# The exact last step of a top-k selection cut into pieces between other VectorE work

## The chip, the cores and the metric

The kernel runs on one core of a Trainium2 chip. The metric is the device time of one execution in microseconds, the median over the runs. TensorE multiplies matrices (in the profile PE, its weight loads PEld), VectorE (DVE) and ScalarE (ACT) work elementwise, GpSimd (POOL) does little here, and SyncE (SP) issues most loads. Each engine works through its own instructions in the order in which they were written, and waits on semaphores for the others.

## The reference, cut to what matters

Two transformer blocks of 1024 tokens and width 1024. The change lies in the second block's mixer, whose four branches share one projection. Branches 0 and 1 are differential attention, branch 2 is a mixture of dilated attentions, branch 3 attends to the 256 keys that an indexer scores highest:

```python
def dsa_attention(q, k, v, iq, ik, iw, table):
    topk = min(TOPK_MAX, S // 4)                    # 256
    def block(args):                                # 128 queries
        logits = einsum('bqhd,bkd->bqhk', iqb, ik) * (IDX_DIM ** -0.5)
        score = einsum('bqhk,bqh->bqk', relu(logits), iwb)
        score = where(kpos <= qpos, score, NEG)
        _, idx = lax.top_k(score, topk)
        ...
        s = where(valid, q @ k[idx] * scale + bias, NEG)
        return softmax(s) @ v[idx]
```

Among equal scores top_k takes the lower index first, so the selection must be exact. For the queries of tiles 0 and 1 (of 128) every admissible key is taken; tiles 2 to 7 need the selection.

## The kernel before

The attention of the four branches is one loop of 64 steps, `for n in range(STEPS2 + 1)`, written once for each engine. Step n is branch n // 16, query tile t = (n % 16) // 2 and half x = n % 2; its scores are 128 x 128 (t + 1), twice (m = 0, 1). So steps 32 to 47 are branch 2 and steps 48 to 63 branch 3, and steps get wider from t = 0 to 7.

TensorE's step n: `scores2(n)` (L1070), `turn2(n - 1, 0)` (L1081, transposes of the weights), fillers, `turn2(n - 1, 1)`, fillers, `values2(n - 1)` (L1098). Fillers are matmuls of other work, put there by the table `fillers()`: projections (L992, L1003), the first half of the output projection (L1015, "out", steps 38 to 44), the memory's keys and values (L1030, L1040). A filler takes one of two PSUM banks, and its result must have been read before the bank is used again. For "out" it is VectorE that reads it (L2459, in `filled`), for the others ScalarE.

ScalarE's step n: copy of turn2(n - 1, 0), exp of (n, 0) in `weigh` (L1709), copy of fillers, copy of turn2(n - 1, 1), exp of (n, 1), and up to step 55 counts of signs for the search (L1756). All its copies are the helper's line L1279.

VectorE's step n: `scored(n, 0)`, `narrow("low")`, `scored(n, 1)`, `narrow("high")` (scored adds the bias and takes the maximum: L2412, or L2407 and L2409 with the selection; narrow is a pass of a search by halving), the fillers' additions of slot 0, `normalise(n, 0)` and `(n, 1)` (L2435 reciprocal, L2437), the additions of slot 1, then `keep_ranked(n)`.

The search finds for each row two neighbouring floats, between which the 256th score lies: tiles 2 to 5 ("low") by step 33, tiles 6 and 7 ("high") by step 56. `keep_ranked` is the exact last step of one tile: it counts the scores at least as large as the bound (`at least`) and larger (`beyond`), both in parts of 256 columns (L2348), derives the value and the number of equals still to be taken (L2350 to L2358), and for each part marks the equals, numbers them by a scan, keeps the first of them and adds those above (L2362 to L2370). L2373 turns the marks into an addend. The table

```python
RANKED_AT = {34: 2, 36: 3, 38: 4, 40: 5, 57: 6, 59: 7}
```

says at the end of which step which tile is done. The result of tile t is wanted by `scored` of step 48 + 2 t.

Of the kernel before, what the change touches and what calls it, by code (L numbers as in the profile page):

```python
# [211 lines left out]
RANKED_AT = {34: 2, 36: 3, 38: 4, 40: 5, 57: 6, 59: 7}  # L212
# [54 lines left out]
class Psum:  # L267
# [20 lines left out]
    def at(self, key):  # L288
        return self.tensor[:, self.bank[key] * 512:8 * 512]
# [48 lines left out]
def program(nc, A, known):  # L338
# [7 lines left out]
    steps = Steps(sems, known)  # L346
# [3 lines left out]
    at = steps.value  # L350
# [118 lines left out]
    def sel(t):  # L469
        return view(SEL_AT[t], (t + 1) * P)  # L470

    def vec(name, i=0, n=1):
        a = VEC0 + VCOL[name] + i
        return S[:, a:a + n]
# [1393 lines left out]
    def vector_program(raw):  # L1868
# [461 lines left out]
        def parts_of(t):  # L2330
            return [(a, min(256, (t + 1) * P - a)) for a in range(0, (t + 1) * P, 256)]

        def keep_ranked(n):

            if n not in RANKED_AT:
                return
            t = RANKED_AT[n]
            j, x, parts = t - 2, sel(t), parts_of(t)
            e.wait_ge(*at(("turned ends", "low" if t < 6 else "high")))
            if t > 2:  # L2340
                e.wait_ge(*at(("sel", t - 1)))
            for name, total, compare in (("at least", at_least, ALU.is_ge), ("beyond", beyond, ALU.is_gt)):
                for p, (a, w) in enumerate(parts):
                    if p:
                        e.wait_ge(*at((name, t, p - 1)))
                    elif name == "beyond":
                        e.wait_ge(*at(("at least", t, len(parts) - 1)))
                    v.tensor_scalar(equal[:, 0:w], x[:, a:a + w], above[:, j:j + 1], total if p else 0.0, compare, ALU.add,  # L2348
                                    accum_out=total).then_inc(*e.step((name, t, p)))
            v.tensor_scalar(is_above, at_least, float(TOPK), None, ALU.is_ge).then_inc(*e.step(("is above", t)))  # L2350
            e.wait_ge(*at(("beyond", t, len(parts) - 1)))
            v.tensor_tensor(beyond, at_least, beyond, ALU.subtract).then_inc(*e.step(("at bound", t)))
            v.tensor_scalar(at_least, at_least, -1.0, float(TOPK), ALU.mult, ALU.add).then_inc(*e.step(("left", t)))
            e.wait_ge(*at(("is above", t)))
            stt(out=rank_value, in0=gap[:, j:j + 1], scalar=is_above, in1=below[:, j:j + 1], op0=ALU.mult, op1=ALU.add).then_inc(
                *e.step(("rank value", t)))
            e.wait_ge(*at(("left", t)))
            stt(out=rank_left, in0=beyond, scalar=is_above, in1=at_least, op0=ALU.mult, op1=ALU.add).then_inc(*e.step(("rank left", t)))  # L2358
            e.wait_ge(*at(("rank left", t)))
            for p, (a, w) in enumerate(parts):  # L2360
                count = prefix[p % 2][:, 0:w]
                v.tensor_scalar(equal[:, 0:w], x[:, a:a + w], rank_value, None, ALU.is_equal).then_inc(*e.step(("equal", t, p)))  # L2362
                e.wait_ge(*at(("equal", t, p)))
                v.tensor_tensor_scan(count, equal[:, 0:w], equal[:, 0:w], prefix[(p - 1) % 2][:, 255:256] if p else 0.0,
                                     ALU.add, ALU.max).then_inc(*e.step(("prefix", t, p)))
                e.wait_ge(*at(("prefix", t, p)))
                stt(out=equal[:, 0:w], in0=count, scalar=rank_left, in1=equal[:, 0:w], op0=ALU.is_le, op1=ALU.mult).then_inc(
                    *e.step(("first equal", t, p)))
                e.wait_ge(*at(("first equal", t, p)))
                stt(out=x[:, a:a + w], in0=x[:, a:a + w], scalar=rank_value, in1=equal[:, 0:w], op0=ALU.is_gt, op1=ALU.add).then_inc(  # L2370
                    *e.step(("selected", t, p)))
                e.wait_ge(*at(("selected", t, p)))
            v.tensor_scalar(x, x, 1.0, -8 * NEG, ALU.subtract, ALU.mult).then_inc(*e.step(("sel", t)))  # L2373

        e.wait_ge(*at("iw"))
        for t, i in INDEX_STEPS:
            for m in range(2):
                h = 2 * i + m
                n = 8 * (t - 2) + h
# [16 lines left out]
        def scored(n, m):  # L2396

            br, t, x = step2(n)
            s = 8 * (n % 5) + 3 * m
            tile, ps, bias = score_tile(n, m), psum.at(("s2", n, m))[:, 0:(t + 1) * P], strip_of(n, m)  # L2400
            e.wait_ge(*at(("strip", br, x if br >= 2 else 0)))
            e.wait_ge(*at(("s2 mm", n, m)))
            if 2 * n + m >= 3:
                e.wait_ge(*at(free(*divmod(2 * n + m - 3, 2))))
            if br == 3 and t >= 2:
                e.wait_ge(*at(("sel", t)))
                v.tensor_tensor(tile, ps, bias, ALU.add).then_inc(*e.step(("biased", n, m)))  # L2407
                e.wait_ge(*at(("biased", n, m)))
                v.tensor_tensor_reduce(out=tile, in0=tile, in1=sel(t), scale=-0.125, scalar=3e38, op0=ALU.add, op1=ALU.min,  # L2409
                                       accum_out=small[:, s:s + 1]).then_inc(*e.step(("max2", n, m)))  # L2410
            else:
                v.tensor_tensor_reduce(out=tile, in0=ps, in1=bias, scale=-0.125, scalar=3e38, op0=ALU.add, op1=ALU.min,  # L2412
                                       accum_out=small[:, s:s + 1]).then_inc(*e.step(("max2", n, m)))
                steps.at["biased", n, m] = steps.at["max2", n, m]

        def combine(n):

            s = 8 * (n % 5)
            e.wait_ge(*at(("exp2", n, 0)))
            e.wait_ge(*at(("exp2", n, 1)))  # L2420
            v.reciprocal(small[:, s + 5:s + 6], small[:, s + 4:s + 5]).then_inc(*e.step(("recip sum2", n)))
            v.reciprocal(small[:, s + 2:s + 3], small[:, s + 1:s + 2]).then_inc(*e.step(("recips", n)))
            e.wait_ge(*at(("recip sum2", n)))
            v.tensor_scalar(small[:, s + 5:s + 6], small[:, s + 5:s + 6], small[:, s + 1:s + 2], neg_lam,
                            ALU.mult, ALU.mult).then_inc(*e.step(("ratio", n)))
            e.wait_ge(*at(("ratio", n)))
            p0 = score_tile(n, 0)
            stt(out=p0, in0=score_tile(n, 1), scalar=small[:, s + 5:s + 6], in1=p0, op0=ALU.mult, op1=ALU.add).then_inc(
                *e.step(("prob", n, 0)))

        def normalise(n, m):

            s = 8 * (n % 5) + 3 * m
            e.wait_ge(*at(("exp2", n, m)))
            v.reciprocal(small[:, s + 2:s + 3], small[:, s + 1:s + 2]).then_inc(*e.step(("recips", n, m)))  # L2435
            e.wait_ge(*at(("recips", n, m)))
            v.tensor_scalar(score_tile(n, m), score_tile(n, m), small[:, s + 2:s + 3], None, ALU.mult).then_inc(  # L2437
                *e.step(("prob", n, m)))
# [14 lines left out]
        def filled(kind, *which):  # L2453

            if kind == "out":
                m, c = which
                x = X[:, m, 512 * c:512 * c + 512]
                e.wait_ge(*at(("out2a mm", m, c)))
                v.tensor_tensor(x, psum.at(("out2a", m, c))[:, 0:512], x, ALU.add).then_inc(*e.step(("x2a", m, c)))  # L2459

        for n in range(STEPS2 + 1):
            if n < STEPS2:
                scored(n, 0)
            narrow("low", n - 1)
            if n < STEPS2:
                scored(n, 1)
            narrow("high", n - 1)
            for piece in FILLERS.get((n, 0), ()):
                filled(*piece)
            if n < 32:  # L2470
                combine(n)
            elif n < STEPS2:
                normalise(n, 0)
                normalise(n, 1)
            for piece in FILLERS.get((n, 1), ()):
                filled(*piece)
            if n == MEM_STEP:
                e.wait_ge(*at("mem rr"))
                for k in range(KD):
                    stt(out=mem[:, k, :], in0=mem[:, k, :], scalar=vec("norm_memkv", k), in1=mem_rr, op0=ALU.mult,  # L2480
                        op1=ALU.mult).then_inc(*e.step(("mem h", k)))
            keep_ranked(n)
            count_least(n)
            if 1 <= n <= 32:
                divide(n - 1)
# [283 lines left out]
    @block.vector  # L2769
    def _(raw):  # L2770
        vector_program(raw)
# [167 lines left out]
```

## Time and profile before

| | us |
|---|---|
| median of 3 runs | 3599.42 |
| lowest, highest | 3598.71, 3608.11 |
| the profiled execution | 3598.85 |
| its span in the trace | 3597.1 |
| TensorE busy | 3436.0 (96%) |
| VectorE busy | 1601.4 (45%) |
| ScalarE busy | 978.1 (27%) |

The profile is of one execution. A timeline row gives start, length, engine, line, operation, operands, the number of merged instructions, and in brackets the idle time of the engine before it and what ended it. The matmuls' ends are modelled; start to start is the surer measure. The loop's steps 32 to 63 lie at 2049 to 2397 us.

### The profile page before, as it was taken

The page shows a single profiled execution, that of the slowest core. Times are in us where ns is not written, and L with a number is a line of the kernel's source. Part 1 is how long each engine was busy: PE and PEld are TensorE (multiplying, and loading weights), DVE is VectorE, ACT ScalarE, POOL GpSimd, SP SyncE. Part 2 cuts the span into 40 slices and gives each one's busy share as a digit, 9 for nine tenths or more (in the row PEclk, how much of TensorE's full clock was granted, in tenths as well). Part 3 has the DMA queues.
Part 4 walks back from the last instruction along what each step waited for, and adds up shares of the span by engine and source line. Part 5 has one row for each costly group of instructions (what it writes and reads, how often), then busy time and mean ns, then how long its engine had stood idle before and what let it go on. Part 6 is the DMA issues. An engine that isn't in the chain of part 4 may idle for free.

```text
span 3597.1 us, 31176 instructions
## 1 busy us (share of the span) xinstructions
PE 3436.0 (96%) x12370; PEld 1812.8 (50%) x12370; DVE 1601.4 (45%) x2938; ACT 978.1 (27%) x2059; POOL 93.6 (3%) x107
## 2 busy tenths in 40 slices
PE   7999999999999999999999999899999999999998
PEld 3556555555456444544566455564444444444443
DVE  2056191143156362552465563654336555253433
ACT  4244112002244111122577744531111000000001
POOL 0000000020000000100000000000110000000000
PEclk9999999999999999999999999899999999999999
DMA  5100121131000101111000101111000111101011
GB/s 209 54 6 13 58 88 62 53 108 38 27 7 13 34 27 53 41 44 41 36 24 30 39 21 56 62 45 44 29 24 35 47 47 35 47 35 47 35 41 65
DMA packets 49903, 163.72 MB, mean 46 GB/s; under 512 B 5296, under 2 KB 8624, under 8 KB 49085
## 3 DMA queue, kind: packets, MB, share of 16 engines
q1 hardware_dynamic: 44890, 145.82, 11.5%
q10 hardware_dynamic: 4868, 15.91, 1.3%
q8 instruction: 98, 1.61, 0.2%
q14 instruction: 47, 0.39, 0.0%
HBM read 157.46 MB, written 11.32 MB: 47 GB/s over the span
## 4 chain that ended last, share of the span: by engine, by line
PE 86%; DVE 7%; ACT 4%; issue 1%; SPq 1%; DMA 0%; POOL 0%; DVEq 0%; ACTq 0%; POOLq 0%
PE ps L551 34%; PE ps L1220 14%; PE ps L580 8%; PE ps L992 5%; PE ps L708 4%; PE ps L1003 2%; PE ps L731 2%; PE ps L887 2%; PE ps L720 2%; PE ps L1015 1%; PE ps L1070 1%; ACT sb L1756 1%; PE ps L1081 1%; DVE sb L2000 1%; PE ps L977 1%; PE ps L1098 1%
## 5 line engine op out<-in xcount | busy, mean ns | idle before, releaser
L551 PE MATMUL ps<-sb 128*128 128x512 f32 (+1 forms) x3088 | 1240.9, 563 | 14.0 <-ACT sb L1559 6.7
L551 PEld LDWEIGHTS ps<-sb 128*128 128x128 f32 x3088 | 589.3, 191 | 659.3 <-issue 633.8
L1279 ACT ACTIVATE sb<-ps 128x512 f32<-128x512 f32 (+10 forms) x709 | 350.6, 511 | 1522.9 <-PE ps L551 467.3
L1220 PE MATMUL ps<-sb 128*128 128x512 f32 x1232 | 531.3, 594 | 2.8 <-DVE sb L2626 2.8
L1220 PEld LDWEIGHTS ps<-sb 128*128 128x128 f32 x1232 | 234.6, 191 | 299.0 <-issue 293.5
L580 PE MATMUL ps<-sb 128*128 128x512 f32 x672 | 291.4, 594 | 2.4 <-ACT sb L1279 1.9
L992 PE MATMUL ps<-sb 128*128 128x512 f32 x512 | 231.3, 599 | 0.0
L580 PEld LDWEIGHTS ps<-sb 128*128 128x128 f32 x672 | 127.3, 190 | 163.2 <-issue 156.1
L1321 ACT ACTIVATE sb<-sb 128x512 f32<-128x512 f32 x128 | 74.7, 610 | 366.0 <-DVE sb L2573 122.5
L2136 DVE SCALAR_TENSOR_TENSOR sb<-sb 128x1310 f32<-128x1310 f32 (+1 forms) x120 | 161.7, 1424 | 0.0
L708 PE MATMUL ps<-sb 96*128 96x512 f32 (+1 forms) x400 | 155.3, 523 | 5.2 <-ACT sb L1468 4.5
L1756 ACT ACTIVATE sb<-sb 128x384 int8<-128x384 f32 (+4 forms) x160 | 152.2, 953 | 2.4 <-DVE sb L2295 0.7
L992 PEld LDWEIGHTS ps<-sb 128*128 128x128 f32 x512 | 94.2, 192 | 107.3 <-issue 106.5
L2000 DVE TENSOR_REDUCE sb<-ps 128x1 f32<-128x1280 f32 (+1 forms) x72 | 98.8, 1372 | 97.4 <-PE ps L708 97.3
L2573 DVE TENSOR_TENSOR sb<-ps,sb 128x512 f32<-128x512 f32 x64 | 44.2, 691 | 216.7 <-PE ps L551 216.7
L1880 DVE SCALAR_TENSOR_TENSOR sb<-sb 128x512 f32<-128x512 f32 (+1 forms) x138 | 88.0, 704 | 110.8 <-ACT sb L1302 86.0
L1003 PE MATMUL ps<-sb 128*128 128x256 f32 x512 | 115.6, 381 | 0.0
L1709 ACT ACTIVATE sb<-sb 128x128 f32<-128x128 f32 (+7 forms) x128 | 98.7, 771 | 62.3 <-DVE sb L2412 33.1
L708 PEld LDWEIGHTS ps<-sb 96*128 96x128 f32 x400 | 71.9, 192 | 78.8 <-issue 73.2
L1003 PEld LDWEIGHTS ps<-sb 128*128 128x128 f32 x512 | 95.6, 190 | 18.0 <-issue 6.2
L720 PE MATMUL ps<-sb 128*128 128x128 f32 x656 | 99.5, 281 | 5.1 <-DVE sb L2017 2.1
L1468 ACT ACTIVATE sb<-ps,sb 128x1280 f32<-128x1280 f32 (+1 forms) x72 | 88.6, 1231 | 48.9 <-DVE sb L2000 48.7
(258 smaller groups left out, 3148.9 us busy)
## 6 DMA issues: line engine op xcount, KB each, us to landing
sb<-in_w_in SPq DMA_DIRECT2D x73, 512.0 KB, 3.3
sb<-in_w_ada SPq DMA_DIRECT2D x48, 512.0 KB, 4.6
sb<-in_w_up SPq DMA_DIRECT2D x44, 512.0 KB, 3.3
sb<-in_w_down SPq DMA_DIRECT2D x24, 384.0 KB, 3.1
sb<-in_w_out SPq DMA_DIRECT2D x16, 512.0 KB, 3.6
sb<-in_w_mkv SPq DMA_DIRECT2D x16, 512.0 KB, 3.3
rows_dram<-vec_dram ACTq DMA_DIRECT2D x1, 6906.0 KB
sb<-rows_dram ACTq DMA_DIRECT2D x6, 1024.0 KB, 5.1
```

The lines of the kernel that those rows point to most:

```text
L551: ins = mm(ps[:, 0:tn], w[:, k, :], src(k, t0, tn), start=(k == 0), stop=(k == nk - 1))
L580: ins = mm(ps[:, 0:512], stationary(k), moving(k), start=(first and k == 0), stop=(k == 3), skip_group_check=not first)
L708: ins = mm(ps[:, b:b + w], qh[0:96, h % 2, t * P:(t + 1) * P], kh[0:96, h, keys0 + b:keys0 + b + w], start=True, stop=True)
L720: ins = transpose(ps[:, (j - g) * P:(j - g + 1) * P], prob[u % 3][:, j * P:(j + 1) * P], ident)
L992: ins = mm(ps[:, 0:512], weights[name][:, k, :], H2[:, k, 512 * c:512 * c + 512], start=(k == 0), stop=(k == KD - 1))
L1003: ins = mm(ps[:, 0:256], H2[:, k, t * P:(t + 1) * P], w[k // 4][:, k % 4, :], start=(k == 0), stop=(k == KD - 1))
L1220: ins = mm(ps[:, 0:512], stationary(k), moving(k), start=(first and k == 0), stop=(k == 3), skip_group_check=not first)
L1279: return act(out, in_, func, scale=scale)
L1709: act(tile, tile, ACT.Exp, bias=small[:, s:s + 1], scale=-1.0, accum_out=small[:, s + 1:s + 2]).then_inc(*e.step(("exp2", n, m)))
L1756: ins = act(out, x, ACT.Sign, bias=bound[:, j:j + 1], scale=sense[:, j:j + 1], accum_out=tally[:, j:j + 1])
L2000: v.tensor_reduce(small[:, s:s + 1], psum.at((l, "s", u))[:, 0:nk], AX.X, ALU.max, negate=True).then_inc(*e.step((l, "max", u)))
L2136: ins = stt(out=out, in0=src, scalar=w, in1=out, op0=ALU.mult, op1=ALU.add)
```

## The change

`keep_ranked(t)` becomes a generator that stops after the `at least` counts, and before each part's marking. A tile of P parts so has P + 2 pieces (tiles 2 and 3 have 2 parts, 4 and 5 have 3, 6 and 7 have 4). `rank_pieces(n, k)` runs up to k pieces of the tile under way, or of the one that RANKED_AT names for step n if it hasn't begun. It is called twice in a step: with 2 ahead of the normalisation, with 1 where keep_ranked stood.

```diff
+        ranking = [None]
+
+        def rank_pieces(n, pieces):
+
+            for _ in range(pieces):
+                if ranking[0] is None and n in RANKED_AT and ("sel", RANKED_AT[n]) not in steps.at:
+                    ranking[0] = keep_ranked(RANKED_AT[n])
+                if ranking[0] is not None and next(ranking[0], "kept") == "kept":
+                    ranking[0] = None
+
-        def keep_ranked(n):
-
-            if n not in RANKED_AT:
-                return
-            t = RANKED_AT[n]
+        def keep_ranked(t):
+
...
                     v.tensor_scalar(equal[:, 0:w], x[:, a:a + w], above[:, j:j + 1], total if p else 0.0, compare, ALU.add,
                                     accum_out=total).then_inc(*e.step((name, t, p)))
+                if name == "at least":
+                    yield
...
             for p, (a, w) in enumerate(parts):
+                yield
                 count = prefix[p % 2][:, 0:w]
...
             for piece in FILLERS.get((n, 0), ()):
                 filled(*piece)
+            rank_pieces(n, 2)
             if n < 32:
                 combine(n)
...
-            keep_ranked(n)
+            rank_pieces(n, 1)
             count_least(n)
```

With the table unchanged the pieces fall as follows (ahead of the normalisation + behind it): tile 2 at step 34 (2 + 1) and 35 (1), tile 3 at 36 (2 + 1) and 37 (1), tile 4 at 38 (2 + 1) and 39 (2), tile 5 at 40 and 41 likewise, tile 6 at 57 (2 + 1) and 58 (2 + 1), tile 7 at 59 and 60 likewise. The instructions of the other engines stand as before.

VectorE from step 57's second scores to step 58's first, in the kernel before (L2409 is the end of the scores, L2437 the normalisation, L2407 the scores of step 58):

```order
L2409 ISA sb<-sb 128x640
...
L2437 TENSOR_SCALAR sb<-sb 128x640
...
L2348 TENSOR_SCALAR sb<-sb 128x256 x3
...
L2358 SCALAR_TENSOR_TENSOR sb<-sb 128x1
L2362 TENSOR_SCALAR sb<-sb 128x256
...
L2362 TENSOR_SCALAR sb<-sb 128x128
...
L2373 TENSOR_SCALAR sb<-sb 128x896
L2407 TENSOR_TENSOR sb<-ps,sb 128x768
```

The same stretch and the beginning of step 58 in the changed kernel, where the lines are 7 to 10 higher (L2447 is the normalisation, L2417 and L2419 the scores):

```order
L2419 ISA sb<-sb 128x640
...
L2355 TENSOR_SCALAR sb<-sb 128x256 x3
...
L2367 SCALAR_TENSOR_TENSOR sb<-sb 128x1
L2445 RECIPROCAL sb<-sb 128x1
L2447 TENSOR_SCALAR sb<-sb 128x640
...
L2372 TENSOR_SCALAR sb<-sb 128x256
...
L2417 TENSOR_TENSOR sb<-ps,sb 128x768
...
L2372 TENSOR_SCALAR sb<-sb 128x256
...
L2447 TENSOR_SCALAR sb<-sb 128x768
```

The counts and the small vectors moved from behind the normalisation of step 57 to ahead of it, one part stayed behind it, and the other three stand in step 58, two ahead of its normalisation and one (not shown) behind it.

VectorE at step 38 in the kernel before (L2295 ends the search's pass, L2459 is a filler's addition, L2412 the scores of step 39):

```order
L2295 SCALAR_TENSOR_TENSOR sb<-sb 128x2
...
L2437 TENSOR_SCALAR sb<-sb 128x512
L2459 TENSOR_TENSOR sb<-ps,sb 128x512
L2348 TENSOR_SCALAR sb<-sb 128x256 x2
...
L2373 TENSOR_SCALAR sb<-sb 128x640
L2412 ISA sb<-ps,sb 128x512
...
L2459 TENSOR_TENSOR sb<-ps,sb 128x512
```

And in the changed kernel:

```order
L2295 SCALAR_TENSOR_TENSOR sb<-sb 128x2
L2355 TENSOR_SCALAR sb<-sb 128x256 x2
...
L2447 TENSOR_SCALAR sb<-sb 128x512
L2469 TENSOR_TENSOR sb<-ps,sb 128x512
L2372 TENSOR_SCALAR sb<-sb 128x256
...
L2422 ISA sb<-ps,sb 128x512
...
L2469 TENSOR_TENSOR sb<-ps,sb 128x512
L2372 TENSOR_SCALAR sb<-sb 128x256
```

The scores of step 39 and the filler's addition behind them now have one part ahead of them in place of the whole of keep_ranked.

## Rows read from the trace of the kernel before

**Rows 1.** The page's fourth part: the chain that ended last, by engine.

```profile
PE 86%; DVE 7%; ACT 4%; issue 1%; SPq 1%; DMA 0%; POOL 0%; DVEq 0%; ACTq 0%; POOLq 0%
```

**Rows 2.** TensorE's waits, 2030 to 2420 us: total, times, longest.

```profile
PE ps L1098 <- ACT sb L1279: 19.6, 11, 7.1
```

**Rows 3.** Timeline of TensorE, steps 39 to 42.

```profile
2113.70 0.66 PE L1081 MATMUL ps<-sb 128*128 128x128 f32 x4
...
2118.06 3.60 PE L1015 MATMUL ps<-sb 128*128 128x512 f32 x8
2125.17 6.43 PE L1015 MATMUL ps<-sb 128*128 128x512 f32 x8 [3.51 <-DVE sb L2459]
...
2156.38 6.17 PE L1015 MATMUL ps<-sb 128*128 128x512 f32 x8 [4.14 <-DVE sb L2435]
```

**Rows 4.** Timeline of TensorE, steps 58 to 62.

```profile
2316.90 1.56 PE L1070 MATMUL ps<-sb 64*128 64x512 f32 x8
2318.39 0.77 PE L1081 MATMUL ps<-sb 128*128 128x128 f32 x5
...
2331.81 2.40 PE L1098 MATMUL ps<-sb 128*64 128x128 f32 x20 [5.20 <-ACT sb L1279]
...
2337.72 0.85 PE L1081 MATMUL ps<-sb 128*128 128x128 f32 x6 [0.56 <-ACT sb L1279]
...
2341.95 1.54 PE L1098 MATMUL ps<-sb 128*64 128x128 f32 x24
2343.43 1.77 PE L1070 MATMUL ps<-sb 64*128 64x512 f32 x8
2345.13 0.87 PE L1081 MATMUL ps<-sb 128*128 128x128 f32 x6
...
2360.71 2.83 PE L1098 MATMUL ps<-sb 128*64 128x128 f32 x24 [7.13 <-ACT sb L1279]
...
2366.51 0.99 PE L1081 MATMUL ps<-sb 128*128 128x128 f32 x7
...
2372.08 1.76 PE L1098 MATMUL ps<-sb 128*64 128x128 f32 x28 [0.36 <-ACT sb L1279]
2373.77 1.99 PE L1070 MATMUL ps<-sb 64*128 64x512 f32 x8
```

**Rows 5.** Timeline of VectorE, steps 38 and 39, and 57 to 61.

```profile
2106.30 0.49 DVE L2437 TENSOR_SCALAR sb<-sb 128x512 f32<-128x512 f32 x1
...
2112.54 0.47 DVE L2348 TENSOR_SCALAR_CACHE_REDUCE sb<-sb 128x256 f32<-128x256 f32 x1
...
2122.55 0.68 DVE L2412 CUSTOM_DVE_ANT_0 sb<-ps,sb 128x512 f32<-128x512 f32 x1
...
2307.60 0.82 DVE L2407 TENSOR_TENSOR sb<-ps,sb 128x640 f32<-128x640 f32 x1 [0.97 <-PE ps L1070]
...
2314.46 0.47 DVE L2348 TENSOR_SCALAR_CACHE_REDUCE sb<-sb 128x256 f32<-128x256 f32 x1
...
2319.25 0.35 DVE L2362 TENSOR_SCALAR sb<-sb 128x256 f32<-128x256 f32 x1
...
2327.99 0.95 DVE L2407 TENSOR_TENSOR sb<-ps,sb 128x768 f32<-128x768 f32 x1
...
2342.05 0.47 DVE L2348 TENSOR_SCALAR_CACHE_REDUCE sb<-sb 128x256 f32<-128x256 f32 x1
...
2347.10 0.35 DVE L2362 TENSOR_SCALAR sb<-sb 128x256 f32<-128x256 f32 x1
...
2356.52 1.08 DVE L2407 TENSOR_TENSOR sb<-ps,sb 128x896 f32<-128x896 f32 x1
```

**Rows 6.** Timeline of TensorE, two other waits and what followed them.

```profile
1964.95 0.33 PE L1081 MATMUL ps<-sb 128*128 128x128 f32 x1 [2.85 <-DVE sb L2450]
1965.11 7.07 PE L1003 MATMUL ps<-sb 128*128 128x256 f32 x32
...
2786.55 33.88 PE L1220 MATMUL ps<-sb 128*128 128x512 f32 x75 [2.60 <-DVE sb L2626]
```

## The prediction, made before the changed kernel ran

> **What bounds the kernel now.** I read the page first. The chain that ended last is TensorE for 86% of the span and VectorE for 7% [rows 1]. So a change that only moves VectorE instructions, as this one does, can win or lose time only where TensorE waits for VectorE. Second, the list of TensorE's waits in 2030 to 2420 us, the stretch of steps 32 to 63 [rows 2]: the largest entry is values2 (L1098) behind a ScalarE copy (L1279), 19.6 us in 11 waits, the longest 7.1. ScalarE is only the messenger: its order puts the copy of the turned weights behind the exp of the next step, and that exp waits for VectorE. Third, the timeline of TensorE at the two places [rows 3, 4], and fourth VectorE's at the same times [rows 5], where the block of keep_ranked (L2348 to L2373) stands: 10.0 us for tile 4 (2112.54 to 2122.55), about 11 for tile 5, 13.5 for tile 6 (2314.46 to 2327.99), 14.5 for tile 7 (2342.05 to 2356.52). Each of these is as long as or longer than TensorE's whole step.
>
> The reader is to see four holes. At step 39 TensorE waits 3.51 us for the filler's addition (the third piece of the step needs a PSUM bank that VectorE has not yet read), and the next 16 matmuls of 512 columns split as 6.43 us for eight, where eight take 3.44 at the full rate [rows 3], 3.60 in the row with its tail. At step 41 the same: 4.14 us and 6.17 for eight. At step 58 values2 waits 5.20 us, at step 60 7.13 us [rows 4]. After each the granted clock is at its lower level (1.2 GHz) for a while, then back at 2.4: this is read from the matmuls' lengths, 2.83 us for 24 of L1098 against 1.54 [rows 4].
>
> **What the change removes.** Nothing: the same instructions in the same number run on VectorE. PE, ScalarE and the DMA queues keep their order.
>
> **What it moves.** In each of the twelve steps 34 to 41 and 57 to 60, up to two pieces now run ahead of the normalisation ("place A") and one behind it ("place B", where all of it was). The two counts and the small vectors are pieces 1 and 2: 4.8 us for tile 6 (2314.46 to 2319.25), 5.05 for tile 7 (2342.05 to 2347.10). A part of 256 columns is 2.2 us: tile 7's four parts and its last L2373 (about 0.6) take 9.42 [rows 5]. The last piece is 2.1 us for tile 6 and 2.8 for tile 7. Tile 4 in its 10.0 us has 1.55 + 2.07 for pieces 1 and 2 by the same prices per count.
>
> **Steps 38 to 42.** I lay the pieces on the clock of rows 3 and 5. Step 38: VectorE is free at 2106.1; pieces 1 and 2 (3.6) end at 2109.7; the two normalisations end at 2111, the filler's addition at 2112.54 as before, piece 3 at 2114.7. The cover: before, normalisation (38, 0) began at 2106.30, and turn2 wants it only at 2113.70 [rows 5, 3], so 7 us lie between; 3.6 fit. Step 39: the scores are ready at 2113.8 and are now read from 2114.7 instead of 2122.55. The filler's addition that TensorE's third piece needs ends at 2118.3, and TensorE wants its bank at 2121.5 (the second piece starts at 2118.06). No wait, so 3.51 goes, and with it the slow eight matmuls (6.43 - 3.44 = 3.0). Together **6.5 us**. Step 40 laid the same way, 6.5 us earlier: pieces 1 and 2 of tile 5 take 3.9, normalisation (40, 0) ends 0.9 us ahead of turn2's wish, the additions 2.5 us or more ahead. 4.14 + 2.73 go: **6.9 us**. Sum 13.4. Steps 34 to 37 (tiles 2, 3) have no hole before, and the shorter counts (2.6 and 2.7 us in place A) go into time that VectorE idled: nothing gained or lost.
>
> **Steps 57 to 61.** Here VectorE itself is short of time. Its steps are now, with start to start times of rows 5 and the same forms: 57: scores 3.21, A 4.79, normalise 1.25, B 2.2, sum 11.4. 58: 3.74, 4.4, 1.48, 2.15, sum 11.8. 59: 3.74, 5.05, 1.48, 2.2, sum 12.4. 60: 4.27, 4.4, 1.66, 2.8, sum 13.2. It starts step 57 at 2307.60, so it ends step 60 at 2356.4 at the earliest, while TensorE without waits would be through it by 2350. So waits come back in smaller form. TensorE has two handles on VectorE: turn2(n, 0) needs normalisation (n, 0), the end of A plus 0.74; and values2(n - 1) starts 3.82 us (768 columns) to 4.19 us (896 columns) after VectorE takes up the scores of n (2327.99 to 2331.81, 2356.52 to 2360.71 [rows 4, 5]), since two exps' worth of ScalarE lies between.
> - Step 58 (starts 2316.90): fills end at 2326.6 (2331.81 less 5.20). VectorE takes the scores at 2319.0, so values2 may go at 2322.8: no wait. It ends at 2327.85.
> - Step 59: scores 1.49 (2316.90 to 2318.39); turn2 and its wait for the copy 0.87 + 0.56, the rest of the turns and the fill 4.23 (2337.72 to 2341.95), to 2335.0. VectorE takes the scores at 2330.8, so values2 may go at 2334.6. It ends at 2336.5.
> - Step 60: scores 1.70, to 2338.2. A ends at 2339.6, normalisation (59, 0) at 2340.3: **wait 2.1**. From here 8.45 (2345.13 to 2353.58, which is 2360.71 less 7.13), to 2348.8; VectorE takes the scores at 2343.2, plus 4.19 is 2347.4: free. Values 1.48, to 2350.3.
> - Step 61: scores to 2352.0; normalisation (60, 0) at 2352.8: **wait 0.8**. Then 5.21 (2366.51 to 2371.72), to 2358.0. VectorE takes the scores at 2356.4, plus 4.19 is 2360.6: **wait 2.6**. Values 1.69, so step 62 starts at 2362.3 against 2373.77.
> That is 11.5 us. Without any wait it would be at 2356.7, 17.1 us.
>
> **The clock after the waits that remain.** Bounds from the nearest rows [rows 6]: after an idle 2.85 us, 32 matmuls of 256 columns took 7.07, the full rate (16 take 3.5); after 2.60 us, 75 of 512 columns took 33.88, where 75 at 0.43 are 32.3: 1.6 lost. So each of the waits of 2.1 and 2.6 costs 0 to 1.7. I take one of the two at 1.7, since the rows fall on both sides. The Trainium skill, "TensorE: Matmul & The Clock Gate", Part 1, says that the monitor runs free of the kernel and that one kernel shows different numbers of slow matmuls from run to run; if so the same wait can be free in one execution and not in the next. One trace can't show that, though these two waits agree.
>
> **The seams.** A piece now ends beside an instruction that does not need it. In the rows a following instruction that doesn't depend starts up to 0.1 us before the last one's written end (L2373 of tile 7 is 0.69 long and starts its successor after 0.61), a dependent one shortly after it. Six seams at 57 to 60 could shorten VectorE's queue by 0.6 us at most, which I leave in the range. The Trainium skill, "VectorE: DVE Perf Modes", "The DRAIN you can't avoid", says that the next instruction waits for the pipe to empty in any case and that a semaphore between costs nothing; by that the seams are worth 0, and by the rows the sum would be 0.6 us larger.
>
> **The sum.** 13.4 + 11.5 - 1.7 = 23.2 us. The profiled execution took 3598.85, its span 3597.1; what lies around the span stays. 3598.85 - 23.2 = 3575.6, and the median of the three runs lies 0.6 above the profiled one, so **3576**. Nothing downstream gives it back by my reading: the weights' loads are issued when TensorE frees a slot, so they move with it, and behind step 63 TensorE is again the chain [rows 1].
>
> **Rivals.**
> - *All holes close.* If VectorE is a little quicker than my sum (seams) or the turns have more slack, steps 60 and 61 have no wait: 13.4 + 17.1 = 30.5, 3568.5. For: only 2.1 and 2.6 us are missing. Against: 48.8 us of VectorE work in four steps in which TensorE has 42. 12%.
> - *VectorE becomes the bound at 57 to 60 more heavily*: the waits of steps 60 and 61 are 3 us each longer (the copy and the fillers' evictions on ScalarE come late too) and each draws the low clock with the full 3 us of rows 3. Gain 23.2 - 6 - 4 = 13, 3586. For: nothing idles there. Against: the waits on VectorE are summed from its own rows. 16%.
> - *The pieces ahead of the normalisation are on TensorE's path* (slower). All of place A, 45 us over the twelve steps, would delay turn2 if the weights were wanted as soon as they are ready. It decides when normalisation (n, 0) ends less than A's 3.6 to 5 us ahead of turn2. Then 45 - 31 = 14 us slower, 3613. Against: 7 us of room at step 38, holes in VectorE's rows of every step. 4%.
> - *It doesn't matter*: the wait for the bank is set by something else than the block, or the gain is given back at the ScalarE-bound short steps 48 to 55: 3599 less at most 8, about 3594. Against: those steps wait on ScalarE's own counts, which move with TensorE. 6%.
>
> **How the numbers follow.** My forecast (3571 to 3581) gets 62%, the rivals 12, 16, 4 and 6. A measurement of this kernel tells from no change what differs by more than 0.3%, 11 us. Faster by more: 62 + 12 + 16 less a little, 88%; within: 8%; slower: 4%. The range that leaves out 2 in 10: 3568 (all holes closed) to 3586 (the heavier bound).
>
> **What would show it.** In the profile after: at steps 39 and 41 the matmuls of L1015 without an idle time and 3.6 us for each eight; the waits of values2 at step 58 gone; a wait of turn2 of about 2 us at step 60, of values2 of 2 to 3 us at step 61; VectorE almost without idle time from step 57 to 60; step 62 some 25 us earlier than before. I am wrong if turn2 waits for L2447 in more than two of the twelve steps (then place A is on the path), or if values2 still waits over 4 us at step 60 or 61.

## The result and the profile after

| | before | changed |
|---|---|---|
| median, us (6 runs each) | 3600.18 | 3575.84 |
| lowest, highest | 3598.65, 3608.11 | 3570.78, 3578.75 |
| span of the profiled execution | 3597.1 | 3576.6 |

The changed kernel takes 0.9927 of the time before, with a 95% interval of 0.9917 to 0.9938: 24.3 us less by the medians, where 3576 was forecast and 23.2 us were summed.

The table of the two stretches, from the start of scores2 of step 38 to that of step 42, and from step 57 to step 62. Columns: stretch, length, busy time (and instructions) of PE, PEld, DVE, ACT, POOL, then TensorE's granted clock as a share of 2.4 GHz, DMA share and GB/s. The kernel before:

```profile
2103.07:2163.73 60.66, 53.01 (x210) 26.78 (x208) 38.25 (x117) 21.72 (x47) 0.00 (x0) 0.89 0.08 27
2306.22:2373.77 67.55, 54.30 (x344) 42.55 (x343) 52.80 (x127) 22.32 (x53) 0.00 (x0) 0.87 0.17 58
```

The changed kernel:

```profile
2108.66:2155.93 47.27, 47.27 (x210) 24.94 (x208) 37.99 (x117) 21.95 (x47) 0.00 (x0) 1.00 0.13 34
2297.62:2353.68 56.06, 49.94 (x344) 39.65 (x343) 52.27 (x127) 22.40 (x53) 0.00 (x0) 1.00 0.23 78
```

The first stretch is 13.39 us shorter and has no idle time of TensorE left; the second is 11.49 us shorter with 6.1 us idle left. VectorE does the same number of instructions in nearly the same time (0.3 and 0.5 us less). The clock is at its upper level throughout, where it was at the lower one for part of both.

TensorE's timeline in the changed kernel. First the place that answers to [rows 3]:

```profile
2119.29 0.66 PE L1081 MATMUL ps<-sb 128*128 128x128 f32 x4
2119.78 3.60 PE L1015 MATMUL ps<-sb 128*128 128x512 f32 x8
2123.22 0.60 PE L1081 MATMUL ps<-sb 128*128 128x128 f32 x4
2123.65 7.03 PE L1015 MATMUL ps<-sb 128*128 128x512 f32 x16
...
2147.72 7.03 PE L1015 MATMUL ps<-sb 128*128 128x512 f32 x16
```

The second and the third filler of steps 39 and 41 run on as 16 matmuls in 7.03 us. Before they were 3.60, a wait of 3.51 or 4.14, and 6.43 or 6.17. Then the place of [rows 4], steps 58 to 62:

```profile
2317.95 1.32 PE L1098 MATMUL ps<-sb 128*64 128x128 f32 x20
...
2327.84 1.77 PE L1070 MATMUL ps<-sb 64*128 64x512 f32 x8
2331.93 0.88 PE L1081 MATMUL ps<-sb 128*128 128x128 f32 x6 [2.32 <-DVE sb L2447]
...
2344.32 0.98 PE L1081 MATMUL ps<-sb 128*128 128x128 f32 x7 [0.77 <-DVE sb L2447]
...
2351.99 1.76 PE L1098 MATMUL ps<-sb 128*64 128x128 f32 x28 [2.47 <-ACT sb L1279]
2353.68 1.99 PE L1070 MATMUL ps<-sb 64*128 64x512 f32 x8
```

values2 of step 58 no longer waits. What is left are three short waits at steps 60 and 61, two for the normalisation (L2447) and one for the exp behind VectorE's scores (a wait of 0.56 us for a copy at step 59 is in both kernels). 28 matmuls of L1098 take 1.76 behind the last, the full rate.

**Why the whole is not the sum of the two stretches.** They give 24.9 us, the two spans differ by 20.5. Step 38 began 5.6 us later in the profiled execution of the changed kernel (2108.66 against 2103.07). So did step 34, the first that the change touches (2066.50 against 2060.90), and from step 34 to step 38 both take the same time, 42.16 and 42.17 us. The changed kernel was 2.3 us later already at step 0 of the loop (1764.73 against 1762.44); no row here shows why. The rest can be seen at 1960 to 2000 us. TensorE's timeline in the kernel before:

```profile
1964.95 0.33 PE L1081 MATMUL ps<-sb 128*128 128x128 f32 x1 [2.85 <-DVE sb L2450]
1965.11 7.07 PE L1003 MATMUL ps<-sb 128*128 128x256 f32 x32
...
1984.87 0.44 PE L1081 MATMUL ps<-sb 128*128 128x128 f32 x2 [2.44 <-DVE sb L2450]
1985.14 7.03 PE L992 MATMUL ps<-sb 128*128 128x512 f32 x16
```

The changed kernel, the same instructions:

```profile
1967.27 0.33 PE L1081 MATMUL ps<-sb 128*128 128x128 f32 x1 [2.85 <-DVE sb L2460]
1967.43 8.76 PE L1003 MATMUL ps<-sb 128*128 128x256 f32 x32
...
1988.89 0.69 PE L1081 MATMUL ps<-sb 128*128 128x128 f32 x2 [2.45 <-DVE sb L2460]
1989.37 8.40 PE L992 MATMUL ps<-sb 128*128 128x512 f32 x16
```

The waits have the same length, 2.85 and 2.44 us. In one execution the full rate follows, in the other the fillers behind the waits take 1.7 and 1.4 us longer, at the lower level. Over nine profiled executions (these two and the seven below) the start of step 34 lies between 2060.90 and 2069.18, with the same instructions ahead of it. Of these 8.3 us, 5.0 are there at step 0 of the loop, and 3.3 come from the two places above, which ran slow together in four of the nine executions and at the full rate together in five. So single executions with the same instructions scatter by several us, and the effect of the change is read from the stretches.

### The profile page after: what moved, and what is told of

It reads as the page before. It is cut to its first block, busy times and chain, and to the rows that moved or that the text cites. A ratio compares the mean times of both kernels' runs of the same rounds, so it can differ in the third digit from the quotient of the medians.

```text
span 3576.6 us, 31190 instructions
## 1 busy us (share of the span) xinstructions
PE 3429.2 (96%) x12370; PEld 1810.5 (51%) x12370; DVE 1601.8 (45%) x2938; ACT 978.8 (27%) x2059; POOL 93.5 (3%) x107
## 4 chain that ended last, share of the span: by engine, by line
PE 87%; DVE 7%; ACT 4%; issue 1%; SPq 1%; DMA 0%; POOL 0%; DVEq 0%; ACTq 0%; POOLq 0%
PE ps L551 34%; PE ps L1220 14%; PE ps L580 8%; PE ps L992 5%; PE ps L708 4%; PE ps L1003 3%; PE ps L731 2%; PE ps L887 2%; PE ps L720 2%; PE ps L1015 2%; ACT sb L1756 1%; PE ps L1070 1%; PE ps L1081 1%; DVE sb L2000 1%; PE ps L977 1%; PE ps L1169 1%
```

## Experiments

All are variants of the changed kernel; its lines are kept. The times of step 38 to 42 and of 57 to 62 come from the starts of scores2 in each profile. e0 to e3 ran on one chip, e4 to e6 on another; each ratio is to the kernel before on the same chip, whose median there was 3599.90 and 3599.53.

| | median us | ratio to before, 95% interval | steps 38 to 42 | steps 57 to 62 |
|---|---|---|---|---|
| before | 3600.18 | | 60.66 | 67.55 |
| changed, again (e0) | 3578.48 | 0.9935 (0.9922 to 0.9947) | 47.27 | 56.06 |
| e1, low tiles only | 3584.86 | 0.9960 (0.9947 to 0.9974) | 47.27 | 67.47 |
| e2, high tiles only | 3592.37 | 0.9974 (0.9965 to 0.9984) | 60.67 | 56.09 |
| e3, all behind | 3583.22 | 0.9951 (0.9939 to 0.9964) | 47.28 | 61.30 |
| e4, whole ahead | 3606.69 | 1.0018 (1.0008 to 1.0027) | 59.45 | 72.23 |
| e5, tile 7 over three steps | 3571.44 | 0.9917 (0.9902 to 0.9932) | 47.27 | 51.51 |
| e6, no ranking | 3572.19 | 0.9917 (0.9902 to 0.9932) | 47.27 | 50.72 |

**The changed kernel again**, beside e1 to e3 on one chip.

> The changed kernel itself, beside the others on one chip. Theory: 0.993 of the kernel before, 24 us less; of it 13.4 us in steps 38 to 42 and 11.5 in steps 57 to 61. What an execution shows ahead of step 38 may differ by some us from the kernel before, since TensorE's clock after its short waits at 1960 to 2030 us is not the same in each execution (the profile of the changed kernel was 5.6 us later there).

It came out 21 us faster than before (3578.48 against 3599.90), with both stretches to 0.01 us as in the first profile. Its step 38 began at 2111.34, the latest of all.

**One part alone.** e1 divides tiles 2 to 5 only, as below; e2 divides tiles 6 and 7 only, with `n >= 57` in the place of `n < 57`:

```diff
-            rank_pieces(n, 2)
+            rank_pieces(n, 2 if n < 57 else 0)
...
-            rank_pieces(n, 1)
+            rank_pieces(n, 1 if n < 57 else 99)
```

> Only tiles 2 to 5 are divided; tiles 6 and 7 run whole behind the normalisation, as before. Theory: the two places are independent, so the gain is 13.4 us, and steps 57 to 61 take 67.5 us as before: 3586 to 3587. Rival (the time won early is given back at the short steps 48 to 55): 3592 or more.

> Only tiles 6 and 7 are divided. Theory: 11.5 us less, 3588 to 3589, steps 38 to 42 as before with the waits of 3.5 and 4.1 us. e1 and e2 add up to the changed kernel's gain within 2 us. Rival (the high tiles gain only because the low ones made room): under 5 us.

Each stretch answers to its own half of the edit and to nothing else: 47.27 and 67.47 in e1, 60.67 and 56.09 in e2. The time from step 42 to step 48 is 80.66 or 80.67 us in all nine profiles. So the time won early is not given back there. By the ratios, e1 gains 0.40% and e2 0.26%, together 0.66%, where the changed kernel gained 0.65% on the same chip: they add up. e1's median is 1 to 2 us better than expected and e2's 3 to 4 us worse, which their stretches don't show (e2's step 38 began at 2106.88, 3.8 us later than that of e1); the scatter ahead of step 34 is of this size, and more than that is not shown.

**The place.** e3 keeps the division and the steps, and puts all three pieces behind the normalisation:

```diff
-            rank_pieces(n, 2)
+            rank_pieces(n, 0)
...
-            rank_pieces(n, 1)
+            rank_pieces(n, 3)
```

> The same pieces at the same steps, but all three behind the normalisation (place B), none ahead of it. Theory: steps 38 to 42 gain the same 13.4. At 57 to 60 VectorE now idles ahead of normalisation (n, 1), which waits for an exp (2.2 us at step 57 in the trace before, less later), about 4 us in all, and values2 of step 61 comes so much later, with a wait of more than 5 us and the low clock behind it: 4 to 7 us more than the changed kernel, 3580 to 3583. Rival (the place in the step does not matter, only the division): the same as the changed kernel within 1 us.

The low tiles gain the same. The high tiles lose 5.24 us of the 11.49, in the expected 4 to 7. The median is 4.7 us above that of e0, at the upper end of the expected 3580 to 3583; the five runs lie 11 us apart (3577.95 to 3589.36), so the stretch is the surer measure. VectorE's timeline at step 57 to 60 shows the idle time (in brackets, the engine that ended it):

```profile
2305.13 0.16 DVE L2445 RECIPROCAL sb<-sb 128x1 f32<-128x1 f32 x1 [2.23 <-ACT sb L1709]
2317.66 0.16 DVE L2445 RECIPROCAL sb<-sb 128x1 f32<-128x1 f32 x1 [0.36 <-ACT sb L1709]
2329.90 0.16 DVE L2445 RECIPROCAL sb<-sb 128x1 f32<-128x1 f32 x1 [0.36 <-ACT sb L1709]
2343.41 0.17 DVE L2445 RECIPROCAL sb<-sb 128x1 f32<-128x1 f32 x1 [0.41 <-ACT sb L1709]
```

and TensorE's timeline the wait that it turns into:

```profile
2328.53 1.54 PE L1098 MATMUL ps<-sb 128*64 128x128 f32 x24 [2.17 <-ACT sb L1279]
2342.05 1.54 PE L1098 MATMUL ps<-sb 128*64 128x128 f32 x24 [1.90 <-ACT sb L1279]
2355.66 3.26 PE L1098 MATMUL ps<-sb 128*64 128x128 f32 x28 [5.23 <-ACT sb L1279]
```

3.4 us idle on VectorE, then a wait of 5.23 us on TensorE with the lower clock behind it (3.26 us for what takes 1.76). This is what the two pieces ahead of the normalisation are good for: they fill the time in which VectorE would wait for the exp of (n, 1). The rival, that only the division matters, falls at the high tiles; at the low tiles it holds.

**The place alone.** e4 doesn't divide; each tile runs whole ahead of the normalisation:

```diff
-            rank_pieces(n, 2)
+            rank_pieces(n, 99)
...
-            rank_pieces(n, 1)
+            rank_pieces(n, 0)
```

> Each tile undivided, at the steps of the kernel before, but whole ahead of the normalisation (place A). Theory: the room of 7 us at step 38 is used up by 10 us, so turn2 waits 3 us at step 39, 6 at 41, about 6.6 at 58 and 7 at 60, with the low clock behind each: the sum of losses is about 33 us against 31 before, 3598 to 3606. So neither place alone brings the gain; the division does. Rival (the gain comes from the place ahead of the normalisation): 3580 or less.

It is 0.18% slower than the kernel before, with a median 0.7 us above the expected 3598 to 3606. TensorE's waits for the normalisation, total, times and longest, in the list of its waits:

```profile
PE ps L1081 <- DVE sb L2447: 27.4, 6, 10.3
```

The four long ones were 3.11, 6.21, 6.69 and 10.28, where 3, 6, 6.6 and 7 were expected. The first bears out the room of 7 us at step 38 that the prediction read from [rows 5, 3], the next two came out as the same sum gave them. The two short ones, 0.28 and 0.83 us at steps 35 and 37, are the price of tiles 2 and 3 run whole ahead of the normalisation, which was not expected; from step 34 to 38 e4 takes 43.40 us, where all others take 42.16 or 42.17. The fourth was my slip, in the expectation of e4: step 59 has one filler where 57 has two, so TensorE is there 2 us sooner, and scores of 768 columns and 14.5 us of ranking stand ahead; the sum is 3.74 + 14.47 + 0.74 less the 8.9 us that TensorE takes from those scores to its wish, which gives 10.1. The first stretch took 59.45, close to the 60.66 before, since one of its two waits left the clock up:

```profile
2123.58 0.66 PE L1081 MATMUL ps<-sb 128*128 128x128 f32 x4 [3.11 <-DVE sb L2447]
2124.07 3.60 PE L1015 MATMUL ps<-sb 128*128 128x512 f32 x8
...
2153.70 1.33 PE L1081 MATMUL ps<-sb 128*128 128x128 f32 x5 [6.21 <-DVE sb L2447]
2154.83 5.79 PE L1015 MATMUL ps<-sb 128*128 128x512 f32 x8
```

Together, e3 and e4 say that the division is what matters at the low tiles, and both division and place at the high ones.

**The sum of VectorE's work.** e5 spreads tile 7 over steps 59 (none ahead, two behind), 60 and 61 (one ahead, one behind):

```diff
-            rank_pieces(n, 2)
+            rank_pieces(n, {59: 0, 60: 1, 61: 1}.get(n, 2))
...
-            rank_pieces(n, 1)
+            rank_pieces(n, {59: 2}.get(n, 1))
```

> As the changed kernel, but tile 7 goes two pieces a step over steps 59 (both behind the normalisation), 60 and 61 (one ahead, one behind), where the changed kernel does three a step at 59 and 60. Theory: VectorE's excess over TensorE at steps 59 and 60 makes the waits of 2.3, 0.8 and 2.5 us that are left. Spread over one more step, the first two go and the third falls to about 1: 4.5 us less than the changed kernel, 3571 to 3572. Rival (the waits come from ScalarE's order, not from VectorE's sum of work): no gain, 3576.

The stretch is 51.51 us, 4.55 less than in the changed kernel. One wait is left:

```profile
2326.49 1.77 PE L1070 MATMUL ps<-sb 64*128 64x512 f32 x8
2328.20 0.87 PE L1081 MATMUL ps<-sb 128*128 128x128 f32 x6
...
2346.10 1.76 PE L1098 MATMUL ps<-sb 128*64 128x128 f32 x28 [1.15 <-ACT sb L1279]
```

So the waits that the changed kernel still has come from VectorE having more to do than TensorE at steps 59 and 60, and not from ScalarE's order. The median, 3571.44, is in the expected 3571 to 3572, 4.4 us below that of the changed kernel's first runs and 7.0 below e0's, in separate sets of runs; the intervals of the ratios overlap, and it is the stretch that shows the gain. By the stretch e5 is the best version found here that still selects.

**The ceiling.** e6 leaves the counts, the derived values and the marking out, so it selects nothing, and keeps one instruction of each tile, behind the normalisation (`rank_pieces(n, 0)` ahead of it and `rank_pieces(n, 99)` behind it). Cut to the main lines:

```diff
             if t > 2:
                 e.wait_ge(*at(("sel", t - 1)))
+            yield
-            for name, total, compare in (...):
...
-            v.tensor_scalar(x, x, 1.0, -8 * NEG, ALU.subtract, ALU.mult)
+            v.tensor_scalar(x, x, 0.0, 0.0, ALU.mult, ALU.mult)
```

> The counts, the derived values and the marking of the six tiles are left out; only the last instruction of each tile remains, with other constants, so nothing is selected. It gives the ceiling: what the exact last step costs at all. Theory: all of the 30.5 to 31 us that the waits and the low clock behind them take in the kernel before, 3568 to 3570, and no more, since TensorE is the bound elsewhere. Rival (VectorE's work costs TensorE time beyond the waits, through the shared memories): less than 3565.

Steps 57 to 62 in e6, in the columns of the first table of stretches:

```profile
2291.78:2342.50 50.72, 49.80 (x344) 39.65 (x342) 27.86 (x53) 22.88 (x53) 0.00 (x0) 1.00 0.22 78
```

VectorE's busy time falls from 52.27 us in the changed kernel to 27.86, and TensorE's matmuls take 49.80 against 49.94. 13.39 + 16.83 = 30.2 us is all that the ranking cost in the kernel before, against 30.5 worked out; e5 leaves 0.8 of it. The median is 27 us below that of before (3599.53 on this chip), at 3572.19 some 2 to 4 us above the expected 3568 to 3570 and above the rival's 3565; the profiled execution of e6 was at 3566.3, 32.6 below that of the kernel before. Of these, 30.2 are the two stretches; against them step 38 began 2.6 us later, and in its favour steps 48 to 57 took 58.18 us, where they took 61.0 to 61.8 in the others, because the 16 matmuls of the memory's sum (L1022) ran at the upper level. In e6:

```profile
2253.87 3.72 PE L1022 MATMUL ps<-sb 128*128 128x256 f32 x16 [1.37 <-ACT sb L1796]
```

and in e5, after the same wait:

```profile
2254.85 6.57 PE L1022 MATMUL ps<-sb 128*128 128x256 f32 x16 [1.37 <-ACT sb L1796]
```

The rival, that VectorE's work slows TensorE beyond the waits, has nothing in these rows for it.

## Why the prediction was right, step by step

- *The holes come from the block, and the bank's wait is VectorE's*: right. e1 and e2 take each half out by itself, e6 all of it.
- *Steps 38 to 42, 13.4 us*: measured 13.39. The waits and the slow matmuls behind them went in full, and the three and four microseconds of place A cost nothing (e3, with nothing in place A, takes 47.28), as the room of 7 us said. e4 shows where that room ends.
- *Steps 57 to 61, 11.5 us*: measured 11.49, with waits of 2.32, 0.77 and 2.47 us where 2.1, 0.8 and 2.6 were laid out. VectorE's queue of the four steps, 48.8 us by the sum, took 48.8, from the scores of step 57 to those of step 61, with no idle time between (the two rows below). The seams gave nothing that can be seen, so the bound of 0.6 us was not needed.

```profile
2299.00 0.82 DVE L2417 TENSOR_TENSOR sb<-ps,sb 128x640 f32<-128x640 f32 x1 [0.96 <-PE ps L1070]
...
2347.79 1.08 DVE L2417 TENSOR_TENSOR sb<-ps,sb 128x896 f32<-128x896 f32 x1
```

- *The clock behind the waits that remain, -1.7 us*: mis-sized. Here it was 0, in both profiles of the changed kernel and in that of e2, which has the same three waits (2.34, 0.77 and 2.46 us) in a stretch of 56.09 us. Such a loss is real in another place: the two waits at 1960 to 2000 us, which the change doesn't touch, cost 3.3 us together in four of nine executions and nothing in five. I had put it in the sum as part of the change, where it belongs to the scatter of both kernels.
- *Nothing is given back later*: right, 80.66 us from step 42 to 48 everywhere, and from step 48 to 57 61.0 against 61.8.
- *The signs*: the waits at steps 39, 41 and 58 are gone, those of steps 60 and 61 have the forecast sizes, and neither condition for being wrong was met (turn2 waits for L2447 twice, values2 at most 2.47 us). Step 62 was to be some 25 us earlier and was 20.1 earlier in the profile: 24.9 from the two stretches and 0.8 from steps 48 to 57, less the 5.6 by which step 34 began later. The start of one step in one execution was a poor sign, and the length of a stretch a good one.
- *The rivals*: "all holes close" is what e5 nearly does (a gain of 13.4 + 16.0), by another table and not by a faster VectorE. "VectorE more heavily the bound" did not occur; e3, with the pieces in the wrong place, has such waits (2.17, 1.90 and 5.23 us, and the lower clock behind the last). "Place A on the path" has its price in e4.

That the forecast of 3576 met the median of 3575.84 is partly luck: the term of 1.7 that was not there and the scatter ahead of step 34 are larger than what was off, and the same kernel's second runs gave 3578.48, 21.4 us below before where the first gave 24.3.

## What to carry to other kernels

An engine that is busy 45% of the span can set the end where a long block of its work stands undivided in its order; compare the block's length with the step of the engine that it feeds, and what is left of the step with the time between when a result is ready and when it is wanted. Divide it into pieces that fit, put them where the engine would wait for another, and sum the engine's work step by step: where it exceeds the other's step, spread it over more steps, which took another 4.55 us here (e5). A hole on TensorE of 3.5 to 4.1 us was worth 1.7 to 1.9 times its length at the low tiles, since the matmuls behind it ran at about half rate.

## What the hardware showed that was not expected

The same wait on TensorE did or did not bring its clock down: 2.85 us was followed by 32 matmuls in 7.07 or in 8.76 us, 1.37 us (after a stretch with many short waits) by 16 in 3.72 in one of the nine profiles and in 6.15 to 6.70 in the other eight, and even 3.11 us left the rate up in e4 where 3.51 cost 3.0 us in the kernel before. The Trainium skill, "TensorE: Matmul & The Clock Gate", Part 1, says that the monitor runs free of the kernel and that one kernel shows other numbers of slow matmuls from run to run; by these rows the trace agrees with the second, and shows it in the middle of a kernel; no row shows the monitor itself. The prediction allowed 0.6 us between one execution and the median; over nine profiles the start of step 34 moved by 8.3.
